# Strassen's scheme for two gate/up chunks of ten feed-forward stages

## What is computed

```python
def swiglu(x, w_gate, w_up, w_down):
    return (jax.nn.silu(x @ w_gate) * (x @ w_up)) @ w_down

x = x + 0.5 * swiglu(rms_norm(x, g), w_gate, w_up, w_down)   # D_MODEL = 1024, D_FF = 2816
```

## Time and profile before

| | |
|---|---|
| median of 3 runs | 3284.26 us |
| span of the profiled execution | 3282.6 us |
| instructions | 38652 |
| PE busy | 3208.3 us, 98% |
| DVE busy | 1832.9 us, 56% |
| ACT busy | 1529.3 us, 47% |
| POOL busy | 183.4 us, 6% |
| bytes moved by DMA | 576.17 MB, mean 176 GB/s |

### The profile page before, as it was taken

How to read it: one execution, slowest core, us unless ns; L and a number is a source line. 1 busy time by engine, 2 the same in 40 slices (tenths; PEclk the granted TensorE clock), 3 DMA queues, 4 the chain that set the end, 5 groups by cost and what they waited for, 6 DMA issues and landing times.

```text
span 3282.6 us, 38652 instructions
## 1 busy us (share of the span) xinstructions
PE 3208.3 (98%) x15901; PEld 2672.8 (81%) x15901; DVE 1832.9 (56%) x2426; ACT 1529.3 (47%) x1935; POOL 183.4 (6%) x297
## 2 busy tenths in 40 slices
PE   8999999979999999999999999999999999999998
PEld 6888888867888888878888888887788788977887
DVE  4467555475555475454575454665655655655545
ACT  4444444455444445444444443466544544565544
POOL 0000000022000000011000000012100000122000
PEclk9999999989999999999999999999999999999999
DMA  6555555523556555555556555654465555744553
GB/s 212 185 187 173 188 179 193 189 95 104 191 175 213 190 170 185 190 195 196 170 180 201 184 188 184 187 167 128 145 194 191 172 187 176 192 131 138 189 192 116
DMA packets 315851, 576.17 MB, mean 176 GB/s; under 512 B 45401, under 2 KB 114092, under 8 KB 315548
## 3 DMA queue, kind: packets, MB, share of 16 engines
q1 hardware_dynamic: 313148, 566.71, 53.7%
q0 software_dynamic: 2384, 6.64, 0.8%
q10 hardware_dynamic: 144, 0.35, 0.0%
HBM read 571.53 MB, written 1.09 MB: 174 GB/s over the span
## 4 chain that ended last, share of the span: by engine, by line
PE 87%; DVE 7%; ACT 4%; issue 1%; DMA 1%; POOL 0%; SPq 0%; DVEq 0%; ACTq 0%
PE up L1866 19%; PE up L1868 19%; PE up L1867 19%; PE acc L1866 8%; PE acc L1868 8%; PE acc L1867 8%; DVE w_lo L1073 3%; ACT w_hi L585 2%; PE up L2245 1%; DVE xT_lo L1189 1%; ACT xT_hi L659 1%; DVE x L1140 0%; ACT units L765 0%; PE acc L2470 0%; PE acc L1963 0%
## 5 line engine op out<-in xcount | busy, mean ns | idle before, releaser
L1073 DVE TENSOR_TENSOR w_lo<-raw,w_hi 128x2048 fp32r<-128x2048 f32 (+1 forms) x543 | 1234.5, 2275 | 1241.8 <-ACT w_hi L585 1239.8
L585 ACT ACTIVATE w_hi<-raw 128x2048 fp32r<-128x2048 f32 (+1 forms) x543 | 1034.0, 1906 | 1347.2 <-PE up L1868 963.2
L1866 PE MATMUL up<-w_hi,xT_hi 128*128 128x512 f32 (+1 forms) x2620 | 1027.2, 392 | 18.1 <-DVE w_lo L1073 6.8
L1868 PE MATMUL up<-w_hi,xT_lo 128*128 128x512 f32 (+1 forms) x2620 | 1019.7, 389 | 0.0
L1867 PE MATMUL up<-w_lo,xT_hi 128*128 128x512 f32 (+1 forms) x2620 | 1019.0, 389 | 0.0
L1866 PEld LDWEIGHTS up<-w_hi,xT_hi 128*128 128x128 f32 x2620 | 492.5, 188 | 126.3 <-DVE w_lo L1073 15.0
L1868 PEld LDWEIGHTS up<-w_hi,xT_lo 128*128 128x128 f32 x2620 | 492.7, 188 | 101.3
L1867 PEld LDWEIGHTS up<-w_lo,xT_hi 128*128 128x128 f32 x2620 | 492.9, 188 | 98.1
L1866 PE MATMUL acc<-w_hi,ff_hi 128*128 128x512 f32 x1232 | 487.3, 396 | 1.2 <-DVE ff_lo L1519 1.2
L1868 PE MATMUL acc<-w_hi,ff_lo 128*128 128x512 f32 x1232 | 480.3, 390 | 0.0
L1867 PE MATMUL acc<-w_lo,ff_hi 128*128 128x512 f32 x1232 | 479.6, 389 | 0.0
(11 more groups left out here) (319 smaller groups left out, 2292.7 us busy)
## 6 DMA issues: line engine op xcount, KB each, us to landing
raw<-in_ffn_down SPq DMA_DIRECT2D x88, 1024.0 KB, 4.9
raw<-in_ffn_gate SPq DMA_DIRECT2D x80, 1024.0 KB, 5.1
raw<-in_ffn_up SPq DMA_DIRECT2D x80, 1024.0 KB, 5.1
raw<-in_ffn_wi SPq DMA_DIRECT2D x80, 1024.0 KB, 5.2
raw<-in_ffn_wo SPq DMA_DIRECT2D x44, 1024.0 KB, 4.9
raw<-in_w_in SPq DMA_DIRECT2D x38, 1024.0 KB, 5.1
raw<-in_conv_w_in SPq DMA_DIRECT2D x24, 1024.0 KB, 5.1
raw<-in_w_in SPq DMA_DIRECT2D x44, 256.0 KB, 4.3
```

Source lines behind the costliest of these rows:

```text
L585: nc.scalar.activation(w_hi[n % RING][:, 0:c], raw[n % RING][:, 0:c], ACT.Copy).then_inc(hi_ready, 1)
L1073: nc.vector.tensor_tensor(w_lo[n % RING][:, 0:c], raw[n % RING][:, 0:c], w_hi[n % RING][:, 0:c].bitcast(F32), ALU.subtract).then_inc(lo_re ...
L1866: pe.matmul(ps, lh, rh, start=start, stop=False)
L1868: return pe.matmul(ps, ll, rh, start=False, stop=stop)
```

## The change

In ten of the twelve feed-forward stages (all but the two that follow the stages `tables` 0 and 1), chunks 2 and 4 of the gate and up product are computed by Strassen's scheme in Winograd's form. The product of a chunk is seen as two by two blocks: the input as token half by feature half (A11, A12, A21, A22, each 128 tokens by 512), the weights as feature half by gate or up (B11 and B21 gate, B12 and B22 up, each 512 by 512, one tile). Seven block products of 12 matmuls (`block_product`) take the place of eight.

The sums of the input side, S1 to S4, are made once per stage by POOL (`fast_operands`), from an input that carries the factor of the normalisation, for which PE spreads `rstd` by a matmul of ones in each of these stages; ACT and DVE split them. The sums of the weight side are made by accumulating DMAs that POOL starts (`fast_sums`): T1 = B11 + B12, T2 = T1 + B22, T3 = B22 + B12, T4 = T2 + B21, each of 1 MB from the weights in memory onto a block that lies in SBUF, one block for B11, T1, T2 and T4 and one for B22 and T3. B11, B21 and B22 are loaded by SP into blocks of their own. The sums of the output side are made by DVE in SBUF and by PE's accumulation in PSUM. Between the block products stand five other tiles (`chunk`), down tiles and one tile of the 256-column tail, in the order B11, tile, B21, T1, tile, B22, T2, tile, T3, tile, T4. All seven are split by ACT and DVE as the other tiles are; a fast chunk so has seven splits where it had four.

The diff, cut to its core:

```diff
+BLOCK_OF = {"B11": 0, "B21": 2, "T1": 0, "B22": 3, "T2": 0, "T3": 3, "T4": 0}
+STEPS_OF = {"v": 1, "u": 2, "c12": 3, "c22": 4, "w": 5, "c21": 6}
...
+        blocks = [carve(5376 + TILE * i, TILE) for i in range(4)]
+        xs = blocks[2].rearrange("p (k n) -> p k n", k=KD)
+        S_raw = blocks[3].rearrange("p (i k n) -> p i k n", i=4, k=4)
+        p1 = xn[:, 0, FW:2 * FW]
...
+        fast_stages = [s for i, s in enumerate(plan) if s[0] == "ffn" and plan[i - 1] not in (("tables", 0), ("tables", 1))]
+
+        def blocks_of(s, c):
+
+            wg, wu, _ = ffn_weights(s)
+            return [kpn(w[512 * h:512 * h + 512, :])[:, :, FW * c:FW * c + FW] for h in range(2) for w in (wg, wu)]
...
+                    def chunk(spacers):
+                        b11, b21, t1, b22, t2, t3, t4 = [(4, FW, None, name) for name in BLOCK_OF]
+                        return [b11, spacers[0], b21, t1, spacers[1], b22, t2, spacers[2], t3, spacers[3], t4]
+
+                    t = wide(wg, 0) + wide(wu, 0) + wide(wg, 1) + wide(wu, 1) + chunk(downs[0:4])
+                    t += wide(wg, 3) + wide(wu, 3) + chunk(downs[4:7] + [tail(0)])
+                    return t + [tail(1)] + downs[7:11]
...
+            def slot_free(r):
+
+                if r >= RING:
+                    sp.wait_ge(lo_ready, loaded[r - RING] + 1)
...
+            def blocks_before(s, n0, j):
+
+                if j == 9:
+                    sp.wait_ge(scale_ready, seen.next(scale_ready))
+                    load_block(s, 2, 0)
+                elif j == 12:
+                    sp.wait_ge(S_summed, seen.next(S_summed, 4))
+                    load_block(s, 2, 2)
+                elif j == 15:
+                    sp.wait_ge(S_lo_ready, seen.next(S_lo_ready))
+                    load_block(s, 2, 3)
+                elif j == 22:
+                    sp.wait_ge(lo_ready, n0 + 18 + 1)
+                    load_block(s, 4, 0)
+                elif j == 24:
+                    load_block(s, 4, 2)
+                elif j == 27:
+                    load_block(s, 4, 3)
...
+                elif every[n][3][0] == "T":
+                    done = sum_ready[every[n][3]]
+                    act.wait_ge(done, seen.next(done, 16))
+                else:
+                    b = block_in[BLOCK_OF[every[n][3]]]
+                    act.wait_ge(b, seen.next(b, 16))
...
+                def first_product():
+                    nc.scalar.activation(p1, up[0][:], ACT.Copy, scale=rstd[:, 0:1]).then_inc(p1_ready, 1)
+
+                def gate_first():
+                    act.wait_ge(ff_prodded, seen.next(ff_prodded))
+                    nc.scalar.activation(ff_gate[:, 0, :], up[0][:], ACT.Silu, scale=rstd[:, 0:1]).then_inc(c11_gated, 1)
+
+                def gate_second():
+                    act.wait_ge(fast_step, seen.next(fast_step, STEPS_OF["c21"]))
+                    nc.scalar.activation(ff_gate[:, 1, :], ff_gate[:, 1, :], ACT.Silu).then_inc(ff_gated, 1)
+
+                def fast(n, c):
+
+                    used()
+                    first_product()
+                    split_hi(n + RING)
+                    hidden_hi(c - 1, 2)
+                    consumed(n + 1)
+                    used()
+                    gate_first()
+                    split_hi(n + 2 + RING)
+                    for j in range(3, 10):
+                        consumed(n + j)
+                    used()
+                    gate_second()
+                    split_hi(n + 10 + RING)
...
+                    consumed(n)
+                    hidden_lo(c - 1, 2)
+                    consumed(n + 1)
+                    consumed(n + 2)
+                    used()
+                    dve.wait_ge(p1_ready, seen.next(p1_ready))
+                    nc.vector.tensor_tensor(second, up[1][:], p1, ALU.subtract).then_inc(fast_step, 1)
+                    split_lo(n + 3 + RING)
+                    consumed(n + 4)
+                    consumed(n + 5)
+                    used()
+                    nc.vector.tensor_tensor(first, up[2][:], p1, ALU.subtract).then_inc(fast_step, 1)
+                    done("u")
+                    nc.vector.tensor_tensor(first, first, up[1][:], ALU.add).then_inc(fast_step, 1)
+                    split_lo(n + 6 + RING)
+                    consumed(n + 7)
+                    used()
+                    done("v")
+                    nc.vector.tensor_tensor(second, second, up[2][:], ALU.add).then_inc(fast_step, 1)
+                    nc.vector.tensor_tensor(ff_gate[:, 1, :], p1, up[2][:], ALU.subtract).then_inc(fast_step, 1)
+                    split_lo(n + 8 + RING)
+                    consumed(n + 9)
+                    done("w")
+                    used()
+                    nc.vector.scalar_tensor_tensor(ff_gate[:, 1, :], up[3][:], rstd[:, 1:2], ff_gate[:, 1, :], ALU.mult,
+                                                   ALU.add).then_inc(fast_step, 1)
+                    dve.wait_ge(c11_gated, seen.next(c11_gated))
+                    nc.vector.tensor_tensor(first, first, ff_gate[:, 0, :], ALU.mult)
+                    dve.wait_ge(ff_gated, seen.next(ff_gated))
+                    nc.vector.tensor_tensor(second, second, ff_gate[:, 1, :], ALU.mult).then_inc(ff_prodded, 1)
+                    split_lo(n + 10 + RING)
...
+                def block_product(n, lh, ll, ps, start):
+
+                    pe.wait_ge(lo_ready, seen.next(lo_ready))
+                    wh, wl = tview(w_hi[n % RING], 4, FW), tview(w_lo[n % RING], 4, FW)
+                    for k in range(4):
+                        pe.matmul(ps, lh[:, k, :], wh[:, k, :], start=start and k == 0, stop=False, skip_group_check=True)
+                        pe.matmul(ps, lh[:, k, :], wl[:, k, :], start=False, stop=False, skip_group_check=True)
+                        last = pe.matmul(ps, ll[:, k, :], wh[:, k, :], start=False, stop=k == 3, skip_group_check=True)
+                    last.then_inc(tile_used, 1)
...
+                    block_product(n, *x_block(0, 0), up[0][:], True)
+                    turn_hidden(c - 1, 4)
+                    if c == 2:
+                        pe.wait_ge(ff_lo_ready, seen.next(ff_lo_ready, 2))
+                    down(n + 1, c - 2, 0)
+                    pe.wait_ge(p1_ready, seen.next(p1_ready))
+                    block_product(n + 2, *x_block(0, 1), up[0][:], False)
+                    if c == 2:
+                        pe.wait_ge(S_lo_ready, seen.next(S_lo_ready))
+                    block_product(n + 3, *s_block(1), up[1][:], True)
+                    down(n + 4, c - 2, 1)
+                    pe.wait_ge(fast_step, base + STEPS_OF["v"])
+                    block_product(n + 5, *s_block(4), up[1][:], False)
+                    pe.wait_ge(ff_lo_ready, seen.next(ff_lo_ready, 2))
+                    block_product(n + 6, *s_block(2), up[2][:], True)
+                    down(n + 7, c - 1, 0)
+                    pe.wait_ge(fast_step, base + STEPS_OF["c12"])
+                    block_product(n + 8, *s_block(3), up[2][:], False)
+                    last_spacer(n + 9)
+                    block_product(n + 10, *x_block(1, 1), up[3][:], True)
...
+                first_pair(n0, FW, gates)
+                pe.wait_ge(diag_ready, seen.next(diag_ready))
+                pe.matmul(acc[3][:, 0:TOK], ones[:], diag[:].rearrange("p t n -> p (t n)"), start=True,
+                          stop=True).then_inc(scale_done, 1)
+                pair(n0 + 2, ups_)
+                pe.wait_ge(ff_gated, seen.next(ff_gated))
+                pair(n0 + 4, gates)
+                turn_hidden(0, 4)
+                pair(n0 + 6, ups_)
+                pe.wait_ge(ff_gated, seen.next(ff_gated))
+                fast(n0 + 8, 2, lambda n: down(n, 1, 1))
+                pe.wait_ge(c11_gated, seen.next(c11_gated))
+                half_pair(n0 + 19, 0, gates)
+                turn_hidden(2, 4)
+                half_pair(n0 + 20, 1, gates)
+                pe.wait_ge(ff_lo_ready, seen.next(ff_lo_ready, 2))
+                pair(n0 + 21, ups_)
+                pe.wait_ge(ff_gated, seen.next(ff_gated, 2))
...
+            def fast_operands():
+
+                pool.wait_ge(scale_ready, seen.next(scale_ready))
+                pool.tensor_tensor(xs, xT_hi[:].bitcast(F32), xT_lo[:].bitcast(F32), ALU.add).then_inc(xs_step, 1)
+                pool.wait_ge(xs_step, seen.next(xs_step))
+                pool.tensor_tensor(xs, xs, rb[:].rearrange("p (o n) -> p o n", o=1).broadcast_to([P, KD, TOK]),
+                                   ALU.mult).then_inc(xs_step, 1)
+                pool.wait_ge(xs_step, seen.next(xs_step))
+                a11, a12 = xs[:, 0:4, 0:P], xs[:, 4:8, 0:P]
+                a21, a22 = xs[:, 0:4, P:TOK], xs[:, 4:8, P:TOK]
+                pool.tensor_tensor(S_raw[:, 0], a21, a22, ALU.subtract).then_inc(S_summed, 1)
+                pool.tensor_tensor(S_raw[:, 2], a21, a11, ALU.subtract).then_inc(S_summed, 1)
```

(95 more changed lines are left out.)

160 lines of the change are left out of this document (141 added, 19 removed).

## The result

The kernel after takes **3294.19 us** (median of 8 runs, 3289.89 to 3297.61), the one before 3284.18 beside it: a ratio of **1.0027 [1.0017, 1.0038]**. That is slower by a little over what can be told from nothing, where 3249 and "faster" were forecast. The profiled execution's span is 3293.0 us against 3282.6.

What follows compares the result with a forecast made beforehand. PE's matmuls were taken as the bound in feed-forward stages. Span: 3282.6 - 54.4 (matmuls) + 5.2 (ones) + 14 (T3 late) = 3247.4 us; median 3249, 8-in-10 range 3233 to 3370.

Steps and rivals of the forecast that it cites:

- the one about SP: Ring loads behind SP's waits for the scale and input sums lose at most one tile of time: costed at nothing.
- POOL's 13 us: POOL's input sums: two operations of 3.8 us and four of 1.27 us, some 13 us, used over 30 us later.
- The deadlines: Transfer time allowed in a fast chunk before PE waits: T3 8.1 us, T2 10.4, T1 9.7, T4 over 13.
- The accumulating transfer: POOL's 1 MB summing DMA: 5.1 plain plus 1.1 for POOL plus 2.8 second pass, shaded to 8.8 us.
- T3 was right: T3's transfer misses its 8.1 us window by 0.7 us per chunk, 20 times, 14 us in all.
- The estimate of 12.3 us: Skill's 6.15 us for 1 MB at half rate for a summing DMA; the second rival's case, making the change slower.
- The ceiling: PE's net gain if nothing waits: 54.4 us of matmuls less 5.2 for the matmul of ones, 49.2 us.
- DVE and ACT: Neither bounds a fast chunk on the mean; busy time rises by 243 us on DVE, about 140 on ACT.
- The half clock: A granted clock below that of before in these stages would make the whole forecast wrong; no size given.
- the second: Rival: weight sums land late, PE waits ahead of T2 and T3; mostly 3290 to 3400 us, priced 98 us; chance 0.33.
- The third: Rival: DVE late, slowed by POOL's sums or misplaced small operations; 10 us lost, 3259 us; chance 0.03.
- The fourth, "no net change": Rival: accumulating transfers of 10.3 to 10.9 us use up the gain; chance 0.06.

Runs made afterwards that it cites:

- the kernel with both edits: Kernel after, with the scaled input made on DVE instead of POOL and the two output sums put ahead of T3's split: 3245.10 us, 0.9879.
- loads held back: Kernel after, with SP waiting for T1 of chunk 2 to land before loading B22 and the two ring tiles behind it: 3324.32 us, 1.0115.
- the burst put back: Scaled input on DVE and output sums ahead of T3's split, but SP holds back chunk 2's B21 and later loads until B11 is split: 3291.93 us, 1.0017.
- the input on DVE: Kernel after, with DVE instead of POOL making the scaled input; POOL keeps the four input sums, nothing left out: 3263.98 us, 0.9936.
- ring tiles: Kernel after, with T1 to T4 loaded unsummed by SP through the ring, no POOL transfers, input sums kept: 3244.74 us, 0.9876.
- the ones later: Scaled input on DVE and output sums ahead of T3's split, plus matmul of ones and scaled input one tile later: 3259.04 us, 0.992.
- the plain transfers: Kernel after, with POOL's four transfers per chunk loading their blocks plainly, without accumulating, so weight sums are left out: 3243.94 us, 0.9873.

## Why the prediction was wrong

**The step that failed** is the one about SP: "those are issued two tiles and more before their split, land in 5.1 us, and lose at most one tile of that: nothing". For the held-back loads themselves that was true; ordinary tiles waited no more than before. I never asked what they would collide with. They are started by the last of POOL's sums, from 2.4 us before T1's transfer to 6 us after its start, whose window was 9.7 us. T1 of chunk 2 then took 12.8 us where I had 8.8. The figure of 8.8 us was one for all the transfers, with nothing on it for five loads that start beside one of them.

**The term behind it** is POOL's 13 us, which was 20.2: 4.61 + 6.54 + 3.24 + 1.29 + 3.23 + 1.30. I had 3.8, 3.8 and 1.27 us from the earlier trace rows. The operations themselves are not much longer than that. POOL's timeline above and DVE's splits in the last part, read together, show it: the second operation ends 4.47 us after a split of DVE has ended (1006.19 to 1010.66), the first and the third short sum 1.17 and 1.16 us after one. The six need 14.0 us in all, and 6.2 us are waits for three splits of DVE, 2.1 us each. I had sized POOL's operations as if it worked alone, and put nothing on its working beside DVE. The last sum, which takes 1.3 us in nine stages, takes 3.2 in the one stage where a split stands ahead of it (least, median and longest, in ns):

```profile
L3137 POOL TENSOR_TENSOR arena<-arena x10: 1287/1297/3219, 57.4 to 3103.5; 128x512 f32<-128x512 f32 x10
```

The short sums put the length of the chain to the test: without the 11 us of the first two, 33 us of span come back. With sums of 13 us B21 would have started some 9.6 us ahead of T1's transfer, further ahead than the 8.4 us of the kernel with both edits, where T1 takes 9.2 us in the median and T2 is in time. That is worked out; no run has it.

The Trainium skill, "GPSIMD Engine Reference", section "3.1 Elementwise — side-by-side cycle accounting", has 4497 ns for an fp32 `tensor_tensor` addition of 2048 numbers. The trace agrees: the first operation takes 4608, and the second, a product, ends 4.47 us after DVE's split.

**The deadlines were right.** My rule that a late T1 passes its delay on to T2, late by the sum of the two transfers less 20.1 us, gives 12.8 + 9.4 - 20.1 = 2.1 us with the measured transfers; PE waited 2.0 in the stage shown. With loads held back the ten stages' medians are 10.9 and 13.8, which gives 4.6, and 4.7 us is the median of the waits. With the burst put back it gives 14.9 + 9.3 - 20.1 = 4.1, and T2's product starts 3.7 us late; there T1's transfer is issued 0.5 us earlier than the 9.2 us ahead of zero that I had. I fed the rule one value for all transfers; it wanted T1's own. (A fast chunk is 41.7 us by my own sum, the value that I used, and not 41.5.)

**The accumulating transfer was right where little lies beside it**: 8.8 us forecast; 8.3 at least, and medians of 8.6 and 8.8 in the two largest groups with the input on DVE. Its parts were right in part by luck. Accumulating adds 3.0 us where I had 2.8 for a second pass of the bytes; that it is a second pass no run shows. POOL's extra was put at 1.1 us, shaded by 0.2, and is 0.5 (plain transfers of 5.6 us against 5.1). **T3 was right** where T1 and T2 were in time: 0.7 us per chunk forecast, 0.9 in chunk 4 and 0.8 with the input on DVE. That 1.4 us of it were an order of DVE's that could be changed, I had in the sum and did not see as avoidable.

The estimate of 12.3 us that rests on the Trainium skill, "Collectives: The Full Stack", section "The bandwidth ceiling: the fold count and why AG ≠ RS ≠ AR", half rate for two source reads, is not borne out as a property of the transfer (8.3 us). That the time came out on the side it spoke for is chance: the transfers were lengthened by the loads beside them.

**The ceiling was 10 us too high**: 49.2 against 39.4. The 54.4 us of PE's matmuls are there (240 fewer). The matmul of ones costs 0.33 us, not 0.52, 1.9 less in all. Against it stand its wait for `diag` in three stages, some 4 us, which I had costed nowhere; 4 us because the products with S lie 0.2312 us apart, not 0.2266 us; and 2.8 us in a stage that the diff doesn't touch. 1 us is left over.

**DVE and ACT** were right on the mean: DVE's busy time rises by 290 us where 243 was forecast, ACT's by 138 against 140. The 47 us more on DVE are splits that take longer beside POOL's operations: the full splits take 1403.5 us in all after the change and 1352.2 with both edits, where POOL does only the short sums. The two input operations that take POOL 4.61 and 6.54 us, DVE's split included in the second, take DVE 2.28 and 2.29.

**The half clock** was named only as something that would make all of it wrong. It is real, follows from the waits, and adds about 8 us in five stages. In two mixing stages the clock was also 0.50 for 6.8 us after the change, with the same waits that left it at 1.00 before, and each of these two stages is 2.9 us longer than before; it comes and goes among the experiments (none with ring tiles, one stage with both edits, both stages with the ones later). With loads held back, where PE waited 3.3 to 6.0 us ahead of T2, it fell in all ten stages. What decides it behind waits of about 2 us stays open.

**The rivals**: the second had the right place, PE's wait ahead of T2 and T3. It named sharing with the ring's loads, but for T3 and T2, where it was T1 that was lengthened; so the delay was T1's own, passed on once, and not 2 us per us. Its price of 98 us was for all twenty chunks, and the ten chunks 4 were never in danger. The third had POOL's sums slow DVE down, and they do, but with the plain transfers, where POOL's operations are the same, no product waits for it. The fourth, "no net change", described the sum and nothing of the mechanism.

## What to carry to other kernels

- A load that is held back costs where it lands: when a change makes a queue wait, write down what the queue will start at the moment of release, and what else is in flight then. Here a transfer with a window of 9.7 us and 8.6 us of its own took 12.8 beside five others.
- Chained transfers (the second starts when the first is consumed) add their delays. The slack of the chain is what counts, and each link needs its own duration in its own surroundings.
- Durations of two engines, each from rows in which it works alone, need not hold side by side. Here POOL's sums and DVE's splits took turns, and 14.0 us of sums became 20.2.
- Before moving loads later to make room, try to make them earlier: here it was two operations on another engine, worth 30 us.

## What the runs showed of the hardware

- **Accumulating DMA**: 1 MB from memory onto a block in SBUF takes 8.3 us at least (8.2 in the run with the ones later), the plain one by the same queue 5.3; POOL's own instruction takes 1.29 us in place of 0.75. Beside two to five plain loads of 1 MB it took 11.2, 12.8, 13.3 and 14.9 us.
- **DVE beside POOL**: a split of DVE and an operation of POOL, each with two operands in SBUF, took turns, each waiting for the whole of the other, and the trace shows the wait as part of the duration. Four splits while POOL worked, and one behind it:

```profile
1002.71 3.48 DVE L1226 TENSOR_TENSOR w_lo<-raw,w_hi 128x2048 fp32r<-128x2048 f32 x1 [3.36 <-ACT w_hi L656]
1008.15 4.66 DVE L1226 TENSOR_TENSOR w_lo<-raw,w_hi 128x2048 fp32r<-128x2048 f32 x1 [1.96 <-ACT w_hi L656]
...
1014.05 3.32 DVE L1226 TENSOR_TENSOR w_lo<-raw,w_hi 128x2048 fp32r<-128x2048 f32 x1
1019.03 3.02 DVE L1226 TENSOR_TENSOR w_lo<-arena,w_hi 128x2048 fp32r<-128x2048 f32 x1 [1.66 <-ACT w_hi L656]
...
1025.37 2.29 DVE L1226 TENSOR_TENSOR w_lo<-raw,w_hi 128x2048 fp32r<-128x2048 f32 x1
```

Set beside POOL's timeline, the four end 2.15, 2.15, 2.15 and 2.14 us after the operation of POOL that runs when they start (it ends at 1004.04, 1010.66, 1015.22 and 1019.91). In the whole trace 40 splits meet an operation of `fast_operands`, and all end 2.14 to 2.16 us after one. It holds the other way too: the short sums take 1.3 us alone and end 1.15 to 1.17 us after a split. Without the two operations ahead of them the first short sum takes 1.28 us and not 3.24, and the fourth takes 3.2, as a split now stands ahead of that one.

The Trainium skill, "SBUF — State Buffer", section "SBUF: two separate sides", says that a DVE operation with two inputs in SBUF and a GpSimd operation that reads SBUF exclude each other for a whole instruction; these rows agree.
